# A product-key expert layer: the last 32 of 256 tokens by gathered expert rows, 224 tokens through all experts

## What is computed

```python
SEQ, D_MODEL, PEER_HEADS, PEER_NKEYS, PEER_TOPK = 256, 1024, 8, 128, 16   # 128*128 experts

q = (xc @ w_query).reshape(T, PEER_HEADS, 2, 128)
s1 = einsum('thd,hnd->thn', q[:, :, 0], sub_keys_1)
s2 = einsum('thd,hnd->thn', q[:, :, 1], sub_keys_2)
v1, i1 = top_k(s1, 16);  v2, i2 = top_k(s2, 16)
cand = v1[..., :, None] + v2[..., None, :]          # 256 candidates of each head
best, pos = top_k(cand, 16)
idx = take_along_axis(i1 * 128 + i2, pos)           # expert numbers
g = softmax(best)
u = expert_u[idx]
act = gelu(einsum('td,thkd->thk', xc, u))
out = einsum('thk,thkd->td', g * act, expert_v[idx])
```

## Time and profile before

| | us |
|---|---|
| median of 3 runs | 1711.76 (1711.26 to 1712.6) |
| span of the profiled execution, first to last instruction | 1710.7 |
| u stage, chunks without gates / with gates | about 243 to 424 / 424 to 634 |
| v stage | about 634 to 983 |
| TensorE, VectorE, ScalarE, GpSimd busy | 1673.7, 977.4, 903.0, 1002.6 |

### The profile page before, as it was taken

How to read it: one execution, slowest core, us unless ns; L and a number is a source line. 1 busy time by engine, 2 the same in 40 slices (tenths; PEclk the granted TensorE clock), 3 DMA queues, 4 the chain that set the end, 5 groups by cost and what they waited for, 6 DMA issues and landing times.

```text
span 1710.7 us, 29415 instructions
## 1 busy us (share of the span) xinstructions
PE 1673.7 (98%) x9272; PEld 1426.3 (83%) x9272; DVE 977.4 (57%) x2113; ACT 903.0 (53%) x1638; POOL 1002.6 (59%) x540
## 2 busy tenths in 40 slices
PE   8989999999999999999999999999999999899998
PEld 7867998888888888888888888978888787788887
DVE  6273489887778885555555557753222376532222
ACT  5565654445454444554455466526555665555554
POOL 4805868888777762000000078528888885578887
PEclk9999999999999999999999999999999999999999
DMA  6624545555444446566555645115555554255553
GB/s 226 176 91 148 206 152 188 190 187 184 163 160 164 158 161 200 191 193 196 190 192 195 217 150 159 50 50 178 189 191 194 170 179 134 88 179 195 189 191 123
DMA packets 83072, 288.16 MB, mean 168 GB/s; under 512 B 9264, under 2 KB 9264, under 8 KB 82480
## 3 DMA queue, kind: packets, MB, share of 16 engines
q1 hardware_dynamic: 82560, 286.10, 51.4%
q10 hardware_dynamic: 432, 1.05, 0.2%
HBM read 285.01 MB, written 2.10 MB: 168 GB/s over the span
## 4 chain that ended last, share of the span: by engine, by line
PE 91%; DVE 4%; ACT 2%; issue 1%; POOL 1%; DVEq 0%; POOLq 0%; ACTq 0%
PE acc L656 14%; PE acc L657 14%; PE acc L658 14%; PE col L954 14%; PE col L958 7%; PE col L1250 7%; PE col L1254 4%; PE col L693 2%; PE col L694 1%; PE col L695 1%; PE mb L970 1%; PE mb L971 1%; PE acc L1169 1%; PE mb L728 1%; ACT hT L1490 1%
## 5 line engine op out<-in xcount | busy, mean ns | idle before, releaser
L2028 POOL TENSOR_TENSOR w_lo<-w_raw,w_hi 128x1024 fp32r<-128x1024 f32 (+2 forms) x394 | 932.1, 2380 | 309.5 <-ACT w_hi L1466 284.3
L1466 ACT ACTIVATE w_hi<-w_raw 128x1024 fp32r<-128x1024 f32 (+1 forms) x539 | 565.7, 1052 | 294.3 <-PE acc L658 240.3
L954 PE MATMUL col<-hT,w_hi 128*128 128x512 f32 x1024 | 259.2, 395 | 0.0
L954 PEld LDWEIGHTS col<-hT,w_hi 128*128 128x128 f32 x1024 | 183.8, 189 | 32.8
L656 PE MATMUL acc<-w_hi,W_hi 128*128 128x512 f32 x512 | 199.4, 389 | 0.4 <-ACT W_hi L1692 0.3
L658 PE MATMUL acc<-w_hi,W_lo 128*128 128x512 f32 x512 | 199.2, 389 | 0.0
L657 PE MATMUL acc<-w_lo,W_hi 128*128 128x512 f32 x512 | 199.2, 389 | 0.0
L2070 POOL TENSOR_SCALAR_AFFINE_SELECT WST<-WST 128x512 f32<-128x512 f32 x1 | 0.7, 693 | 319.8 <-DMA WST<-in_gmlp_w 319.8
L2765 DVE TENSOR_TENSOR w_lo<-w_raw,w_hi 128x1024 fp32r<-128x1024 f32 x128 | 156.1, 1221 | 1.1 <-ACT w_hi L1466 1.1
L958 PEld LDWEIGHTS col<-hT,w_lo 128*128 128x128 f32 x1024 | 139.7, 190 | 10.1
L3012 DVE TENSOR_REDUCE mb<-col 128x256 f32<-128x512 f32 x64 | 44.8, 699 | 180.7 <-PE col L1254 180.7
(11 more groups left out here) (592 smaller groups left out, 3078.5 us busy)
## 6 DMA issues: line engine op xcount, KB each, us to landing
w_raw<-in_expert_u SPq DMA_DIRECT2D x128, 512.0 KB, 3.3
w_raw<-in_expert_v SPq DMA_DIRECT2D x128, 512.0 KB, 4.3
w_raw<-in_w_mlp SPq DMA_DIRECT2D x128, 512.0 KB, 3.3
w_raw<-in_w_in SPq DMA_DIRECT2D x24, 512.0 KB, 3.9
w_raw<-in_w_qkv_o SPq DMA_DIRECT2D x24, 512.0 KB, 3.9
w_raw<-in_w_query SPq DMA_DIRECT2D x16, 512.0 KB, 3.3
w_raw<-in_w_gate SPq DMA_DIRECT2D x16, 512.0 KB, 3.3
w_raw<-in_w_qkv_e SPq DMA_DIRECT2D x12, 512.0 KB, 3.4
```

The costliest lines, as they stand in the source:

```text
L954: mm(both, wh[:, k, :], hT[:, :, k, :], start=k == 0, stop=k == KD - 1, skip_group_check=True)
L1466: f(w_hi[:, s, 0:w], w_raw[:, s, 0:w], ACT.Copy).then_inc(sem(f"hi{s}"), 1)
L2028: g.tensor_tensor(w_lo[:, s, 0:w], w_raw[:, s, 0:w], w_hi[:, s, 0:w].bitcast(F32), ALU.subtract).then_inc(sem(f"lo{s}"), 1)
```

## The change

The last 32 tokens (`SPARSE`) leave the dense path, which keeps 224 (`DENSE`).

- All dense matmuls of the u stage have 2 x 224 = 448 or 224 columns; the gates take 56 steps, the first half of u 72 chunks; `BETWEEN` is 1910.
- In the v stage the weights are stationary (8 blocks of the features) and the gated activations move, high and low part side by side: 8 matmuls of 448 columns and 8 of 224 in a chunk, into all 8 banks of PSUM. `W` holds both parts. The sum comes out turned, so the last chunk goes bank by bank, ScalarE copies the low half of each bank out, VectorE adds the halves (`outT`), TensorE turns them back (`expert_sums`) and VectorE adds the residual, which stays in `X`; the spill is gone.
- The 32 tokens are laid out four times over the 128 partitions (`PARTS` = 4), each copy with 32 (`SLOTS`) of the token's 128 experts. VectorE packs expert numbers, gate weights and the norm's factor; ScalarE's queue spreads them and the tokens by DMA in the gate steps (`sparse_inputs` at step 2, `sparse_tokens` at step 6).
- In the v stage GpSimd gathers 64 tiles of 128 rows (512 KB each), 32 of u and 32 of v, by indirect DMA into two buffers; VectorE takes a dot product of each u tile with the tokens (`tensor_tensor_reduce`, spread over chunks 4 to 62), ScalarE applies gelu, and VectorE adds each v tile times its weight to `sparse_sum` (`scalar_tensor_tensor`, chunks 70 to 122). Two matmuls with `fold` sum the four copies.
- `POOL_LO` = -1: no chunk of the v stage has its low part made by GpSimd, as before.

```diff
+SPARSE = 32
+DENSE = SEQ - SPARSE
+PARTS = P // SPARSE
+SLOTS = PE_H * TOPK // PARTS
-BETWEEN = 2180
+BETWEEN = 1910
+STEPS = DENSE // QUAD
+HALF = NKEYS - STEPS
 FILLED_AT = HALF - 4
-STEPS = SEQ // QUAD
+DOT_AT = [4 + 60 * j // SLOTS for j in range(SLOTS)]
+WEIGHTS_AT = 68
+ROW_AT = [70 + 54 * j // SLOTS for j in range(SLOTS)]
+TILES_AT = DOT_AT + ROW_AT
+SPARSE_GELU = 17
+POOL_LO = -1
...
                 for k in range(KD):
-                    mm(both, wh[:, k, :], hT[:, :, k, :], start=k == 0, stop=k == KD - 1,
+                    mm(both, wh[:, k, :], hT[:, :, k, 0:DENSE], start=k == 0, stop=k == KD - 1,
                        skip_group_check=True)
                 lo_in(U0 + q, r)
                 for k in range(KD):
-                    m = mm(both[:, 0, :], wl[:, k, :], hT_hi[:, k, :], start=False,
+                    m = mm(both[:, 0, :], wl[:, k, :], hT_hi[:, k, 0:DENSE], start=False,
...
+            def v_chunk(q, r, first=False, last=False):
+                n = r * 4 + q
+                opening, closing = first and q == 0, last and q == 3
+                pe.wait_ge(sem("W_hi"), n + 1)
+                pe.wait_ge(sem("W_lo"), n + 1)
+                hi_in(V0 + q, r)
...
+                def wide(b):
+                    mm(both_of(v_bank[b]), w_hi[:, slot, b * P:(b + 1) * P], gated, start=opening,
+                       stop=closing, skip_group_check=True)
+                def narrow(b):
+                    return mm(v_bank[b][:, 0:DENSE], w_lo[:, slot, b * P:(b + 1) * P], gated[:, 0, :],
+                              start=False, stop=closing, skip_group_check=True)
+                if closing:
+                    for b in range(8):
+                        wide(b)
+                        m = narrow(b)
+                        if b < 7:
+                            m.then_inc(sem("v_full"), 1)
+                else:
+                    for b in (6, 7, 4, 0, 1, 2, 5, 3) if opening else range(8):
+                        if opening:
+                            bank_ready(b)
+                        wide(b)
+                    lo_in(V0 + q, r)
+                    for b in range(8):
+                        m = narrow(b)
+                m.then_inc(sem(f"used{slot}"), 1)
...
+            def expert_sums():
+                def turn_out(t, n):
+                    wide_ = P if t == 0 else P - SPARSE
+                    for b in range(4):
+                        m = pe.transpose(acc[2 * t + n][0:wide_, b * P:(b + 1) * P],
+                                         outT[:, 4 * n + b, t * P:t * P + wide_], ident[:, :])
+                    return m
+                pe.wait_ge(sem("out_sum"), 4)
+                turn_out(0, 0).then_inc(sem("outX"), 1)
+                pe.wait_ge(sem("fold"), 1)
+                pe.wait_ge(sem("tile_used"), 2 * SLOTS)
+                for n in range(2):
+                    mm(acc[2 + n][P - SPARSE:P, :], fold[:, :], sparse_sum[:, n * 512:(n + 1) * 512],
+                       start=True, stop=True, skip_group_check=True)
+                pe.wait_ge(sem("out_sum"), 8)
+                turn_out(0, 1).then_inc(sem("outX"), 1)
...
             for s in range(STEPS - 1):
+                if s == 2:
+                    sparse_inputs()
+                if s == 6:
+                    sparse_tokens()
                 keep_gates(s)
...
+            def expert_tile(i):          # GpSimd
+                j, name = i % SLOTS, "u_rows" if i < SLOTS else "expert_v"
+                if i >= 2:
+                    pool.wait_ge(sem("tile_used"), i - 1)
+                g.indirect_dma_start(
+                    expert_rows[i % 2][:, :], None, ins[name],
+                    bass.IndirectOffsetOnAxis(ap=sparse_in[:, j:j + 1].bitcast(U32), axis=0)).then_inc(
+                    sem(f"tile_in{i % 2}"), 16)
...
+            def expert_tile(i):          # VectorE
+                j, rows_ = i % SLOTS, expert_rows[i % 2]
+                dve.wait_ge(sem(f"tile_in{i % 2}"), 16 * (i // 2 + 1))
+                if i < SLOTS:
+                    x = v.tensor_tensor_reduce(rows_[:, :], rows_[:, :], sparse_h[:, :], 1.0, 0.0,
+                                               ALU.mult, ALU.add, sparse_dot[:, j:j + 1])
...
+                    x = v.scalar_tensor_tensor(out=sparse_sum[:, :], in0=rows_[:, :],
+                                               scalar=sparse_w[:, j:j + 1], in1=sparse_sum[:, :],
+                                               op0=ALU.mult, op1=ALU.add)
+                x.then_inc(sem("tile_used"), 1)
+            for n in range(NKEYS):
+                r, q = n // 4, n % 4
+                if n + 2 < NKEYS:
+                    gated_lo(n + 2, (n + 2) % 4)
+                if q != POOL_LO:
                     weight_lo(V0 + q + AHEAD, r)
...
+                for i in range(2 * SLOTS):
+                    if TILES_AT[i] == n:
+                        expert_tile(i)
+            for b in range(8):
+                dve.wait_ge(sem("out_lo"), b + 1)
+                v.tensor_tensor(outT[:, b, :], v_bank[b][:, 0:DENSE], outT_lo[:, b, :],
+                                ALU.add).then_inc(sem("out_sum"), 1)
```

## The result

Median 1684.33 us (1683.25 to 1685.33, 4 runs) against 1711.51 (1710.95 to 1712.6, 4 runs) for the kernel before on the same chip: ratio 0.9841, 95% interval 0.9827 to 0.9855. The kernel is 27 us faster, where 65 had been forecast. The profiled execution's span (of the four after, the fastest) went from 1710.7 to 1681.5 us, -29.2, at a mean granted clock of 0.99.

What follows compares the result with a forecast made beforehand. TensorE was taken as the bound: number of matmuls times their rate. Terms -27.3 - 8.2 - 29.0 - 3.5 + 2.0 + 0.5 = -65.5 on a span of 1710.7, plus 1.1 outside, gave 1646 us; range 1640 to 1690.

Steps and rivals of the forecast that it cites:

- Wide: u stage: 1024 matmuls of 512 columns become 448, 26.7 ns less each: -27.3 us.
- narrow: u stage: 1024 matmuls of 256 columns become 224, at a floor of 0.1117 us against 0.1197: -8.2 us.
- gates: Gate steps: 56 for 64, at 0.44 us of TensorE a step: -3.5 us.
- ScalarE's issues: Gate steps 2 and 6: nine DMA issues on ScalarE, mostly hidden, may delay a gelu and the next gates: +0.5 us.
- For v, 319.9 us was to be left: v stage turned: 1024 matmuls of 448 columns and 1024 of 224, a chunk from 2.72 to 2.494 us: -29.0 us.
- Two buffers ... hidden. It exceeds the 319 us from G = 7.6: v stage: 64 tiles cost 32 x (G + 1.3) plus 35 us, hidden at G = 4.3, over 319 us from 7.6.
- G: v stage: the time of one gather, taken as 4.3 us.
- R2: v stage: gathers arrive late; G over 9.6 us makes it slower, 11 gives 1755 us. Chance 0.10, of which 0.07 slower.
- R3, the port: v stage: issuing a gather holds VectorE; +37 us at 1 us each (1683), slower from 1.45. Chance 0.12, 0.03 slower.
- 57 chunks are placed in the search before and 65 now, against 60 and 68: Top-16 search in u: u chunks placed during it, against those where its result is needed; counted as hidden work.
- R1: v stage: VectorE or the DMA queue falls behind at times; 1655 to 1690 us, say 1665. Chance 0.15.
- The turned sum: End of v: the last residual add ends some 4.1 us past the last matmul instead of 2.1: +2.0 us.

Runs made afterwards that it cites:

- run 5: Changed kernel with each gather replaced by a plain transfer of the same size from the same queue: 1665.63 us, ratio 0.9734.
- run 7: Changed kernel with all gathers kept, but VectorE's 64 tile operations over 8 columns in place of 1024: 1663.85 us, ratio 0.9710.
- run 3: Changed kernel with four buffers in place of two for the gathered expert_v rows: 1669.92 us, ratio 0.9748.
- run 2: Changed kernel with GpSimd's block masks made after the 34th gather, not between the second and third: 1677.79 us, ratio 0.9803.
- run 1: Changed kernel with 67 sums of u columns allowed among the top-16 search steps in place of 65: 1682.51 us, ratio 0.9838.
- run 11: Run 4's three edits, with 68 sums placed, the picks' transposes two u chunks later and the packing behind the first one-hot maps: 1656.17 us, ratio 0.9674.
- Run 9: Changed kernel without gathers and with the 64 tile operations cut to 8 columns: 1660.12 us, ratio 0.9711.
- run 8: Changed kernel without gathers, the 64 tile operations kept at full size on zero-filled buffers: 1660.28 us, ratio 0.9711.
- run 4: Changed kernel with three edits together (67 sums placed, block masks later, four buffers for gathered expert_v rows): 1658.80 us, ratio 0.9685.
- run 6: Changed kernel with every gather led by the indices 0 to 127 in place of the picks: 1683.99 us, ratio 0.9833.

## Why the prediction fell short, step by step

- **The rates: right.** Wide -27.3, narrow -8.2, gates -3.5 (with +0.5 for ScalarE's issues, -38.5) stand against -30.4 measured, and 7.6 of the difference is stall 1. For v, 319.9 us was to be left and the dense part alone took 322.2 (2.51 a chunk, not 2.494: +2).
- **"Two buffers ... hidden. It exceeds the 319 us from G = 7.6": the step that failed, rival R2.** G was taken as 4.3 us, the landing of a load; it measured 7.8: by the medians of runs 5 and 7, 5.5 for a plain transfer beside the loads, 0.4 more for one by index, and 1.9 more beside VectorE's low parts. And the sum was made over the whole stage. Made for the second half, a tile is due every 54/32 x 2.50 = 4.22 us, two buffers give 8.44, and G may be 8.44 - 1.28 = 7.2 at most; in the first half 60/32 x 2.50 x 2 - 1.30 = 8.1. So 7.8 fits the first half, where PE was full from 640 to 680 us, and not the second. Runs 3, 5 and 7 show it from three sides: room for more gathers, G down to 5.5, G down to 5.9, and each time the second half is full. The price was more than the average sum gives (35 + 32 x 9.1 = 326 us for v, measured 345.3), as the stage stands still in the slow half without catching up in the other, and the clock falls behind the longest halts (3.12 and 2.35 us).
- **R3, the port: named, but in the wrong direction.** It asked what a gather costs VectorE. VectorE's tiles kept 1.22 and 1.28 us throughout; it was GpSimd that was held beside VectorE's low parts, 1.98 for 0.94 us, and with it the landing (run 7). The Trainium skill ("SBUF — State Buffer", Who interferes with whom) has both halves of it: a VectorE operation with two SBUF inputs is in the way of a GpSimd instruction that reads SBUF, and not of one that only writes. The prediction had left that condition out. The traces agree: the gather, which reads its indices there, went to 1.98 us, while 61 of the 64 plain transfers of run 5 started beside the same low parts and took 0.53 to 0.58. The hold of the instruction is 1.04 us of the 1.9; how the other 0.9 us of landing come about stays open.
- **The masks: left out.** No term dealt with what stands in GpSimd's queue between the second gather and the third. It cost some 7 us at the start of v, 5.7 over the stage (run 2). GpSimd was idle for nearly all of v (busy 2.63 of 310 us in the earlier trace rows), and what it still did there, ahead of that window, was not asked.
- **"57 chunks are placed in the search before and 65 now, against 60 and 68": the count was right, the place was not.** All 65 are used up twelve steps before the end. But run 1 shows that two more sums alone don't help: VectorE is behind at the picks. With the transposes of the picks two chunks later, and the packing behind the first maps, the u stage gains 4.2 us (run 11).
- **R1, VectorE or the DMA engines behind in v: wrong as a bound.** Run 9 against run 8 clears VectorE. For the engines, 343 GB/s went through from 840 to 880 us of run 4, with PE busy for all of the 40 us; `expert_v` landed after 5.5 us (6.2 in run 4, 4.3 before), and the ring hid it. Its range of 1655 to 1690 held the time for another reason, which is luck.
- **The turned sum: +2.0 forecast, +4.7 measured.** Three low parts stand ahead of the sums in VectorE's queue, and the fold's matmuls take 1.90 us where "up to 1.0 us" had been allowed:

```profile
946.47 3.49 DVE L2914 TENSOR_TENSOR w_lo<-w_raw,w_hi 128x1024 fp32r<-128x1024 f32 x3
949.87 1.28 DVE L2961 TENSOR_TENSOR outT<-acc,outT_lo 128x224 f32<-128x224 f32 x4
951.79 1.90 PE L1055 MATMUL acc<-sparse_sum,fold 128*32 128x512 f32 x4
```

The ledger: of the 36 us between forecast and measurement, 23.1 go with the gathers in the v stage (345.3 - 322.2: 8.0 in its first part, nearly all of it the masks, and 15.1 in the second), 7.6 are the stall at the picks, 2.7 the tail, and 2.3 the dense v rate. The first of these is the least firm: in run 1 the same v stage took 4.6 us less.

## What to carry to other kernels

Work that is moved off TensorE in many small pieces must be priced by its longest loop, not by its busy time: buffers x interval against landing + use, for each phase by itself. A transfer fetched by index is not a load of the same size. In this kernel the index itself cost 0.4 us of landing (5.9 for 5.5), and what VectorE ran beside GpSimd's instruction 1.9; four buffers hid both. And before a new chain is put on a queue, read what that queue already has to do between its links.

## What was not expected of the hardware

- An indirect transfer of 128 rows of 4 KB landed after 7.8 us in the median, a plain one from the same queue after 5.5. Rows in order or scattered: 7.9 to 8.1 and 7.8. A gather whose instruction did not start beside a VectorE low part landed after 5.85 (run 7).
- The copy of 32x4 elements that packs the scale took 0.17 us in eight of the twelve profiles of the changed kernels and 2.26 to 2.34 in four. In those it had started behind a GpSimd low part and ended with it, as in run 7:

```profile
425.58 2.34 DVE L2804 COPY sparse_pack<-rstd 32x4 f32<-32x4 f32 x1
```

```profile
425.49 2.40 POOL L2137 TENSOR_TENSOR w_lo<-w_raw,w_hi 128x1024 fp32r<-128x1024 f32 x1 [0.36 <-ACT w_hi L1542]
```

  Ahead of the gates TensorE then waits 2.44 us (runs 2, 6 and 7), and the u stage took 362.5 to 363.8 us, counted from its own first matmul, against 360.8. It may be part of why runs of one kernel spread by up to 12.6 us here (1675.63 to 1688.18 in run 1), where the kernel before spread by 2; that was not tested.
- In the rows shown, each halt of TensorE of 3 to 5 us was followed by matmuls at the lower clock level: eight of 448 columns took 3.33 to 3.35 us and not 1.80. Such a halt costs 1.5 to 3.0 us beyond itself (3.0 is the 7.6 of stall 1 less its 4.56 of idle time). Length alone does not decide it: in run 2 the matmuls behind a halt of 3.40 us kept the full level (granted clock 1.00 from 899.2 to 904 us), and in the changed kernel those behind one of 2.35 us fell to 0.50 (903.1 to 906). What decides it no run here shows.

```profile
899.17 1.05 PE L1013 MATMUL acc<-W,w_hi 128*128 128x448 f32 x4 [3.40 <-ACT W L1803]
```
